# A hybrid decoder step on one core: 384 of 1056 tokens take their expert rows by indirect DMA, 672 stay dense, and the gates are stored by expert tile, key and token

## The chip, the cores and the metric

The kernel runs on one core of a Trainium2 chip. The metric is the device time of one execution in microseconds (us). Tensors are float32. Where this text says TensorE, VectorE, ScalarE, GpSimd and SyncE, the profile says PE, DVE, ACT, POOL and SP; PEld is TensorE's weight load.

## What is computed

One inference step of a decoder layer, for 1024 prompt tokens and 8 x 4 sample tokens (N = 1056), D = 1024. Three branches (a short convolution, a gated delta rule, a memory attention) are merged; then a product-key expert layer follows. The change is in that last layer alone:

```python
q = (xb @ w_q).reshape(blk, PEER_HEADS, 2, PEER_D_HALF)          # 8 heads
s = jnp.einsum('nhpd,phkd->nhpk', q, sub_keys)                   # 2 x 128 key scores
sv, si = lax.top_k(s, PEER_TOPK)                                 # 16 of each
...
eidx = jnp.take_along_axis(cidx, ti, axis=-1)                    # 16 of 16384 experts per head
gates = jax.nn.softmax(tv, axis=-1)
u = jnp.take(u_tab, eidx, axis=0)
act = jax.nn.gelu(jnp.einsum('nd,nhkd->nhk', xb, u), approximate=False)
coef = gates * act
y = jnp.einsum('nhk,nhkd->nd', coef, jnp.take(v_tab, eidx, axis=0))
```

So each token uses 8 x 16 = 128 rows of `u_tab` and 128 rows of `v_tab` (16384 x 1024 each), and the output is the residual plus y, normalised.

## The kernel before

Everything up to the expert layer (start-up, projections, attention, delta rule, merge) runs first and is not touched. The expert layer is dense: for all 128 tiles of 128 experts the kernel multiplies the tile's u rows with all 1056 tokens, applies Gelu, multiplies by a gate that is zero where the expert was not chosen, and multiplies with the tile's v rows. Every product is split into a rounded high part and a low part and takes three passes (high x high, high x low, low x high). The tokens go in three chunks of 352 columns (`NCH`, `CH`), so a tile costs 8 (`KT`) x 3 chunks x 3 passes = 72 matmuls of 128x352 on either side, 144 in all.

The layer has three stages.

- **Routing** (`top_experts`): for each of the 8 heads PE forms two query products (72 matmuls each, `product`, L2745), the scores (L2756), and, in between, the u product of two expert tiles (`act_tile`, `act_chunk`, L2572) whose Gelu values go to DRAM (`tmp_acts`). DVE finds the top 16 with max, find-index and match-replace instructions (L2872 to L2963), and POOL turns ranks into keys (L2689 to L2705). Twenty tiles are done here (`ROUTE_TILES`).
- **Spreading the gates** (`spread_gates`): for every token DVE writes two one-hot matrices, by second key (L3062) and by first key times gate (L3063), 128x128 each; PE multiplies them (`unit`, L3083, four tokens at a time), ACT copies the result out (L3104), and after every 48 tokens SP stores the block `tmp_gates[block, key, key, token]` (L3132), in which a partition's 128 x 48 values lie together. A round is two blocks, 24 units; 11 rounds do 1056 tokens and four u tiles each (`SPREAD_TILES` = 44).
- **Experts** (`experts`): 64 tiles have their Gelu values in DRAM (STASH), 64 are computed here (LIVE). A `turn` does two live u products and four v tiles in two `values` calls of two tiles (L3265). SP loads a tile's gates in 48-token pieces (L3200), the stashed values (L3206) and v rows (L3212); ACT rounds (L3320, L3325) and applies Gelu (L3333); DVE multiplies by the gate (L3389), forms the low parts (L3394, L3398) and adds the finished banks to `yT` (`sum_up`, L3405). At the end PE transposes the sums, ACT and DVE normalise, SP stores.

The u rows come in as rows of the table and must be transposed: `load_u` fetches 32x32 blocks with four DMAs per tile (L2546, runs of 128 B), `turn_u` transposes on DVE into PSUM (L2561), `raise_u` rounds (L2585) and `cut_u` subtracts (L2605).

Everything is ordered by hand: each engine runs its own program in order, and semaphores tie them. `next_u` on SP asks for a u tile as soon as its slot is free, and in the spreading stage stands on the same queue as the gate stores.

## Time and profile before

| | |
|---|---|
| time, median of 3 runs | 5763.18 us (5760.07 to 5764.72) |
| span of the profiled execution | 5757.6 us |
| PE busy | 5567.8 us (97%) |
| DVE busy | 3314.0 us (58%) |
| ACT busy | 1316.0 us (23%) |
| POOL busy | 854.3 us (15%) |
| moved by DMA | 584.45 MB, 102 GB/s over the span |

The profiled execution's own time is its span, 5757.6 us, from the first to the last instruction; the runs are about 5.6 us above it. Busy times are unions over an engine's instructions. Matmuls overlap in the records (each lasts about twice its distance to the next), so the cost of one is the distance between starts or a group's length divided by its count.

### The profile page before, as it was taken

Reading aid. Unit: us, or ns where it says so; the run is one execution under the profiler, and the core shown is the slowest. Engines: PE = TensorE matmul, PEld = TensorE weight load, DVE = VectorE, ACT = ScalarE, POOL = GpSimd, SP = SyncE. Lnnn points to the kernel's source line nnn. Section 1 sums busy time; section 2 is a strip of 40 time slices with the busy share of each in tenths; the row PEclk is TensorE's granted clock in tenths of the full one; section 3 lists DMA queues with packets and bytes.
Section 4 is the critical chain, followed back from the end, with each engine's and each line's share of the span. In section 5 each row is a group of like instructions: output and inputs, shape, how many; then the busy total and the mean of one; then the engine's idle time right before and its main releaser. Section 6 shows DMA issues by size and latency. Waiting matters only on the chain. (4 is left out here: it accounts for less than half of the span.)

```text
span 5757.6 us, 95894 instructions
## 1 busy us (share of the span) xinstructions
PE 5567.8 (97%) x35846; PEld 5444.1 (95%) x35846; DVE 3314.0 (58%) x7740; ACT 1316.0 (23%) x2393; POOL 854.3 (15%) x550
## 2 busy tenths in 40 slices
PE   8999999998998998999999998999999999999999
PEld 6999998986888997999999998999999999999998
DVE  3236402123766354799778885666666666666665
ACT  3013211122333013222333332112111112111122
POOL 0332323321221333355000000000000000000000
PEclk9999999999998998999999999999999999999999
DMA  4222224343111444222455666333443334443332
GB/s 159 63 63 92 97 88 112 110 154 111 49 45 60 140 123 125 63 63 53 126 154 147 167 158 172 89 89 91 96 101 89 89 89 93 102 94 89 89 89 83
DMA packets 1220496, 584.45 MB, mean 102 GB/s; under 512 B 915240, under 2 KB 1158952, under 8 KB 1217381
## 3 DMA queue, kind: packets, MB, share of 16 engines
q1 hardware_dynamic: 928800, 453.31, 30.1%
q10 hardware_dynamic: 290400, 124.94, 8.1%
q0 software_dynamic: 1152, 4.19, 0.3%
q8 instruction: 101, 1.65, 0.1%
q14 instruction: 43, 0.35, 0.0%
HBM read 410.77 MB, written 171.59 MB: 101 GB/s over the span
## 5 line engine op out<-in xcount | busy, mean ns | idle before, releaser
L3405 DVE TENSOR_TENSOR yT<-yT,ex_y 128x352 f32<-128x352 f32 x1512 | 787.9, 521 | 779.1 <-PE ex_y L3265 779.1
L2572 PE MATMUL ea_banks<-h_high,ea_uT_high 128*128 128x352 f32 x3072 | 1006.9, 328 | 22.6 <-PEq L3026 10.2
L2572 PE MATMUL ea_banks<-h_high,ea_uT_low 128*128 128x352 f32 x3072 | 990.5, 322 | 0.0
L2572 PE MATMUL ea_banks<-h_low,ea_uT_high 128*128 128x352 f32 x3072 | 989.2, 322 | 0.0
L3265 PE MATMUL ex_y<-ex_c_high,w_mb_high 128*128 128x352 f32 x3024 | 976.0, 323 | 4.9 <-DVE yT L3405 4.9
L3265 PE MATMUL ex_y<-ex_c_low,w_mb_high 128*128 128x352 f32 x3024 | 973.1, 322 | 0.0
L3265 PE MATMUL ex_y<-ex_c_high,w_mb_low 128*128 128x352 f32 x3024 | 971.8, 321 | 0.0
L2572 PEld LDWEIGHTS ea_banks<-h_high,ea_uT_high 128*128 128x128 f32 x3072 | 580.0, 189 | 23.7 <-issue 15.4
L2572 PEld LDWEIGHTS ea_banks<-h_low,ea_uT_high 128*128 128x128 f32 x3072 | 581.3, 189 | 0.0
L2572 PEld LDWEIGHTS ea_banks<-h_high,ea_uT_low 128*128 128x128 f32 x3072 | 579.5, 189 | 0.0
L3265 PEld LDWEIGHTS ex_y<-ex_c_high,w_mb_high 128*128 128x128 f32 x3024 | 568.4, 188 | 5.2 <-DVE yT L3405 5.2
L3265 PEld LDWEIGHTS ex_y<-ex_c_low,w_mb_high 128*128 128x128 f32 x3024 | 568.6, 188 | 0.0
L3265 PEld LDWEIGHTS ex_y<-ex_c_high,w_mb_low 128*128 128x128 f32 x3024 | 568.4, 188 | 0.0
L120 PE MATMUL p_in<-h_high,w_in_high 128*128 128x352 f32 x1536 | 495.5, 323 | 0.0
L120 PE MATMUL p_in<-h_low,w_in_high 128*128 128x352 f32 x1536 | 492.3, 320 | 0.0
L120 PE MATMUL p_in<-h_high,w_in_low 128*128 128x352 f32 x1536 | 491.8, 320 | 0.0
L3320 ACT CAST w_mb_high<-w_mb_raw 128x1024 fp32r<-128x1024 f32 x126 | 126.3, 1050 | 1398.5 <-PE ex_y L3265 1394.9
L120 PEld LDWEIGHTS p_in<-h_low,w_in_high 128*128 128x128 f32 x1536 | 288.6, 188 | 0.0
L120 PEld LDWEIGHTS p_in<-h_high,w_in_high 128*128 128x128 f32 x1536 | 288.1, 188 | 0.0
L120 PEld LDWEIGHTS p_in<-h_high,w_in_low 128*128 128x128 f32 x1536 | 287.8, 187 | 0.0
L3062 DVE TENSOR_SCALAR w_mb_raw<-iota,yT 128x128 f32<-128x128 f32 x704 | 197.4, 280 | 136.8 <-PE sg_ps L3083 135.5
L3063 DVE TENSOR_SCALAR w_mb_raw<-iota,yT 128x128 f32<-128x128 f32 x704 | 241.4, 343 | 0.0
(497 smaller groups left out, 9461.7 us busy)
## 6 DMA issues: line engine op xcount, KB each, us to landing
ex_gate<-tmp_gates SPq DMA_DIRECT2D x128, 528.0 KB, 6.2
w_mb_raw<-in_peer_v SPq DMA_DIRECT2D x128, 512.0 KB, 5.6
w_in_raw<-in_w_in SPq DMA_DIRECT2D x88, 512.0 KB, 3.8
ea_u_raw<-in_peer_u SPq DMA_DIRECT2D x268, 128.0 KB, 4.2
tmp_acts<-ea_coef ACTq DMA_DIRECT2D x64, 528.0 KB, 2.7
tmp_gates<-yT SPq DMA_DIRECT2D x11, 3072.0 KB, 9.4
tmp_gates<-sg_out SPq DMA_DIRECT2D x11, 3072.0 KB, 9.5
ex_kept<-tmp_acts SPq DMA_DIRECT2D x64, 528.0 KB, 7.0
```

Of the source, the lines that this page charges most:

```text
L120: last = pe.matmul(banks[0:rows, n, 0:CH], a[:, kk, 0:rows], b[:, kk, chunk(n)], start=(kk == 0 and a is wt.high[s] and b is high), stop=( ...
L2572: last = pe.matmul(acts.banks[:, n, 0:CH], a[:, c, :], b[:, c, chunk(n)], start=(c == 0 and a is acts.uT_high[s] and b is high), stop=(c = ...
L3062: dve.tensor_scalar(second_key[s][:, u, :], k["iota"][:, :], now[:, 1, at:at + 1], None, ALU.is_equal)
L3063: last = dve.tensor_scalar(first_key[s][:, u, :], k["iota"][:, :], now[:, 0, at:at + 1], now[:, 2, at:at + 1], ALU.is_equal, ALU.mult)
L3265: last = pe.matmul(ps_y[:, n, 0:CH], x[:, c, :], y[:, chunk(n)], start=(s == 0 and x is wt.high[0] and y is c_high[kind][0]), stop=(s == 1 ...
L3320: act.copy(v_high[s][:, :, :], v_raw[:, s, :, :]).then_inc(v_high_made, 1)
L3405: dve.tensor_tensor(at, at, ps_y[:, n, 0:CH], ALU.add).then_inc(summed, 1)
```

## The change

It splits the tokens. The first `GT` = 384 (three tiles of 128, one token per partition) leave the dense layer; the other `ND` = 672 stay in it in two chunks of 336 (`DC`, `CD`). For the 384 tokens the 128 expert numbers of each are kept as an index, and for slot j of a token tile one indirect DMA on POOL's queue fetches 128 rows of 4 KB, one per partition. DVE takes a dot product with the token's own row for u, and adds gate x Gelu x row for v. That is 3 x 128 u gathers and 3 x 128 v gathers; the 128 u gathers of the third token tile run in the spreading stage, the other 640 in the expert stage (20 in each of 32 turns, five row buffers).

Besides: u comes from a table that the host lays out transposed (`peer_uT`), so DVE's transposes and the four-part loads go; four instead of two u tiles are done per head (`HEAD_TILES`), 36 tiles in the routing stage and 28 in seven spreading rounds; a spreading unit's two one-hots of four tokens are one DVE instruction of 1024 elements, and POOL multiplies the first keys by the gates; `tmp_gates` is now `[expert tile, key, token]`; and the expert loop is 32 turns, in which the v products of the two stashed tiles and of the two live tiles of the turn before are summed in one bank before `sum_up` adds 672 columns.

The core of the diff (`SUMMED` is the token tile whose dots are made while spreading):

```diff
+G = 3
+GT = G * P
+ND = N - GT
+DC = 2
+CD = ND // DC
-ROUTE_TILES = 2 * H + 4
-SPREAD_TILES = 44
+HEAD_TILES = 4
+ROUTE_TILES = HEAD_TILES * H + 4
+SPREAD_TILES = 28
...
+def gather(pool, table, index, t, slot, row, landed):
+    pool.indirect_dma_start(row, None, table, bass.IndirectOffsetOnAxis(ap=index[:, t, slot:slot + 1], axis=0)).then_inc(landed, 16)
...
-    for j in range(SUB):
-        eng.dma_start(acts.u_raw[j * BLOCK:(j + 1) * BLOCK, s, :].rearrange("r (b c) -> r b c", c=BLOCK), rows[j]).then_inc(acts.u_in[s], 16)
+    eng.dma_start(acts.u_raw[:, s, :], io["peer_uT"][ds(e, 1), :, :].rearrange("o p c -> p (o c)")).then_inc(acts.u_in[s], 16)
...
@@ spread_gates, DVE
-                    for u in range(UN):
-                        at = r * UN + u
-                        dve.tensor_scalar(second_key[s][:, u, :], k["iota"][:, :], now[:, 1, at:at + 1], None, ALU.is_equal)
-                        last = dve.tensor_scalar(first_key[s][:, u, :], k["iota"][:, :], now[:, 0, at:at + 1], now[:, 2, at:at + 1],
-                                                 ALU.is_equal, ALU.mult)
+                    dve.tensor_tensor(keys[s], all_keys, own_keys, ALU.is_equal).then_inc(hot_made, 1)
+                    if r % (per_chunk * DC) == per_chunk:
+                        e, half, s = tile_of(i, r // (per_chunk * DC))
+                        cut_u(dve, acts, e + 1, 1 - s)
...
+                    for m in dots_after(r, first):
+                        dot(i, m, first)
@@ spread_gates, POOL (new)
+                for r in range(units):
...
+                    pool.wait_ge(hot_made, i * units + r + 1)
+                    pool.tensor_tensor(first_key, first_key, over_columns(chosen[:, 2, at:at + UN]), ALU.mult).then_inc(hot_weighed, 1)
+                    for m in dots_after(r, i == 0):
+                        if base + m + RING < P:
+                            pool.wait_ge(row_used, base + m + 1)
+                            gather_next(base + m + RING)
@@ spread_gates, ACT (every tile, at its first chunk)
-                            raise_u(act, acts, e + 1, 1 - s, 3 * e + 48)
+                            raise_u(act, acts, e + 1, half + s, 1 - s)
@@ spread_gates, SP
-                    sp.dma_start(tmp["gates"][ds(2 * i + bs, 1), :, :, :].rearrange("o j i n -> j (o i) n"), out[bs]).then_inc(stored[bs], 16)
+                    sp.dma_start(tmp["gates"][:, :, ds(2 * BT * i + bs * BT, BT)].rearrange("i j n -> j i n"), out[bs]).then_inc(stored[bs], 16)
@@ experts, SP
-                sp.dma_start(gate[:, slot, :].rearrange("p (b n) -> p b n", n=GATE_BLOCK),
-                             tmp["gates"][:, :, ds(tile_of(kind, g, s), 1), :].rearrange("b j o n -> j b (o n)")).then_inc(gate_in[slot], 16)
+                sp.dma_start(gate[:, s, :], tmp["gates"][ds(tile, 1), :, :].rearrange("o j n -> j (o n)")).then_inc(gate_in[s], 16)
@@ experts, POOL (new)
+                if nth >= RING:
+                    pool.wait_ge(row_used, nth - RING + 1)
...
+                gather(pool, table, gt.index, t, EACH * g + j, row[nth % RING], row_in[nth % RING])
@@ experts, DVE (new)
+                if m < U_ROWS:
+                    t, j = m // EACH, m % EACH
+                    dve.tensor_tensor_reduce(out=of, in0=of, in1=gt.h_row[t], scale=1.0, scalar=0.0, op0=ALU.mult, op1=ALU.add,
+                                             accum_out=dots[:, t, j:j + 1]).then_inc(row_used, 1)
+                else:
+                    t, j = (m - U_ROWS) % G, (m - U_ROWS) // G
...
+                    dve.scalar_tensor_tensor(out=gt.sum_row[t], in0=of, scalar=coefs[:, t, j:j + 1], in1=gt.sum_row[t],
+                                             op0=ALU.mult, op1=ALU.add).then_inc(row_used, 1)
@@ experts, ACT: the live coefficients of the turn before
+                act.wait_ge(l_weighed, 2 * g + s + 1)
+                if s == 0:
+                    act.wait_ge(multiplied, KT * (g + 1))
+                act.copy(l_high[s][:, :], acts.coef[:, s, :]).then_inc(l_high_made, 1)
```

Three places show what the program now issues. The first is SP's queue in a spreading round, around the store of the first block: before,

```order
L2546 DMA ea_u_raw<-in_peer_u 32x32x32
L3131 ISA
L3132 ISA
L3132 DMA tmp_gates<-yT 128x6144
L2546 ISA
L2546 DMA ea_u_raw<-in_peer_u 32x32x32
```

and with the change,

```order
L2584 DMA ea_u_raw<-in_peer_uT 128x1024
L3224 ISA
L3225 ISA
L3225 DMA tmp_gates<-yT 128x128x48
L2584 ISA
L2584 DMA ea_u_raw<-in_peer_uT 128x1024
```

The place is the same, but the store is 128x128 runs of 48 values, where it was one run of 6144 per partition, and the next u tile stands right behind it.

The second is POOL's queue at the start of the spreading stage, where it had nothing before (`picks` holds the gates and one of three row buffers, L3120 is the multiplication by the gates):

```order
L2576 DMA yT<-in_peer_u,gt_index 128x1024 x2
L2576 DMA picks<-in_peer_u,gt_index 128x1024
L3120 TENSOR_TENSOR w_mb_raw<-w_mb_raw,picks 128x512 x2
L2576 DMA yT<-in_peer_u,gt_index 128x1024
L3120 TENSOR_TENSOR sg_keys<-sg_keys,picks 128x512
L2576 DMA yT<-in_peer_u,gt_index 128x1024
```

Three gathers go ahead; after that gathers and multiplications alternate.

The third is DVE at the start of a turn of the expert loop (L3389 weighs by the gate, L3398, L3394 and L2605 are low parts): before,

```order
L3389 TENSOR_TENSOR ex_gate<-ex_gate,ea_coef 128x1056
L3397 ISA
L3398 TENSOR_TENSOR w_mb_low<-w_mb_raw,w_mb_high 128x1024
L3397 REGISTER_ALU
L3398 TENSOR_TENSOR w_mb_low<-w_mb_raw,w_mb_high 128x1024
L3382 ISA
L3389 TENSOR_TENSOR ex_gate<-ex_gate,ex_kept 128x1056
```

and with the change,

```order
L3569 TENSOR_TENSOR ex_l_low<-ea_coef,ex_l_high 128x672
L3593 ISA
L3597 ISA yT,ex_dots<-yT,h_high_plain 128x1024
L3597 ISA ex_dots 128x1
L3572 ISA
L3573 TENSOR_TENSOR w_mb_low<-w_mb_raw,w_mb_high 128x1024
L3572 REGISTER_ALU
L3573 TENSOR_TENSOR w_mb_low<-w_mb_raw,w_mb_high 128x1024
```

The turn begins with the live low parts of the turn before, and a dot product, which is two instructions (L3597, the second of one element), stands ahead of the v tiles' low parts.

## Rows read from the trace of the kernel before

**Rows 1.** Busy time of each engine by stretch: routing, spreading, start, loop and end of experts.
```profile
core 0: us, PE busy (x) PEld busy (x) DVE busy (x) ACT busy (x) POOL busy (x), PEclk, DMA share, GB/s
2261.00:2763.00 502.00, 466.39 (x2923) 458.53 (x2923) 417.66 (x1955) 118.52 (x231) 220.11 (x102) 0.96 0.29 63
2763.00:3506.00 743.00, 742.01 (x5278) 742.04 (x5279) 598.27 (x2255) 259.21 (x485) 0.00 (x0) 1.00 0.58 152
3506.00:3556.00 50.00, 31.28 (x169) 30.57 (x168) 16.11 (x17) 10.42 (x17) 0.00 (x0) 0.86 1.05 288
3556.00:5711.00 2155.00, 2155.00 (x13514) 2155.00 (x13513) 1370.68 (x2067) 394.63 (x559) 0.00 (x0) 1.00 0.39 92
5711.00:5757.00 46.00, 32.49 (x221) 30.93 (x219) 24.91 (x44) 13.29 (x28) 0.00 (x0) 0.93 0.26 95
```

**Rows 2.** The chain that ended last, two neighbouring pieces: start us, length us, what.
```profile
4024.75 11.47 PE ea_banks L2572 x72
4036.22 22.96 PE ex_y L3265 x144
```

**Rows 3.** Source L2954 (once per key and head): duration ns, first and last start.
```profile
L2954 DVE TENSOR_TENSOR picks<-iota,tk_rank x16: 2550/2556/2560, 2373.6 to 2741.9; 128x2304 f32<-128x2304 f32 x16
```

**Rows 4.** Groups by line in the routing stage: busy us, mean ns of one.
```profile
L2756 PE MATMUL tk_ps<-tk_keysT,tk_qT 128*128 (+1 forms) x288 | 34.7, 275 | 0.0
```

**Rows 5.** Timeline of DVE in the expert loop: start us, length us.
```profile
4025.23 1.25 DVE L3389 TENSOR_TENSOR ex_gate<-ex_gate,ex_kept 128x1056 f32<-128x1056 f32 x1
4026.40 2.35 DVE L3398 TENSOR_TENSOR w_mb_low<-w_mb_raw,w_mb_high 128x1024 fp32r<-128x1024 f32 x2
4028.67 1.25 DVE L3389 TENSOR_TENSOR ex_gate<-ex_gate,ea_coef 128x1056 f32<-128x1056 f32 x1
```

**Rows 6.** Timeline of DVE: an addition from PSUM, and a scalar-tensor-tensor.
```profile
5727.89 0.51 DVE L3463 TENSOR_TENSOR yT<-yT,ea_banks 128x352 f32<-128x352 f32 x1
5728.31 0.52 DVE L3463 TENSOR_TENSOR yT<-yT,ex_y 128x352 f32<-128x352 f32 x1
...
170.78 1.28 DVE L753 SCALAR_TENSOR_TENSOR conv_out<-conv_in,tap_now,conv_out 128x1024 f32<-128x1024 f32 x1
171.98 0.25 DVE L755 SCALAR_TENSOR_TENSOR conv_out<-conv_in_s,tap_now,conv_out 128x32 f32<-128x32 f32 x1
```

**Rows 7.** Source L3372: how long reading an accumulator out takes on ACT.
```profile
L3372 ACT ACTIVATION_READ_ACCUMULATOR ea_coef<-ea_t x3: 192/193/194, 5724.7 to 5748.0; 128x1 f32 x3
```

**Rows 8.** DMA by 2 us: v rows of 4 KB alone, then u and gate pieces; columns of Rows 1.
```profile
4036.00:4038.00 2.00, 2.00 (x15) 2.00 (x14) 0.52 (x1) 0.47 (x1) 0.00 (x0) 1.00 1.00 379
...
4030.00:4032.00 2.00, 2.00 (x15) 2.00 (x14) 2.00 (x3) 1.39 (x2) 0.00 (x0) 1.00 0.94 139
```

**Rows 9.** DMA queues: packets, MB, share of 16 engines; and the gates' store, KB, us to landing.
```profile
q1 hardware_dynamic: 928800, 453.31, 30.1%
q0 software_dynamic: 1152, 4.19, 0.3%
tmp_gates<-yT SPq DMA_DIRECT2D x11, 3072.0 KB, 9.4
```

**Rows 10.** POOL: a plain DMA of 128 rows of 4 KB, a multiplication, short copies.
```profile
L913 POOL DMA_DIRECT2D tmp_ym<-at_o x8: 844/844/992, 1239.0 to 1289.9; - x8
L1919 POOL TENSOR_TENSOR dp_qkv<-dp_qkv,dp_root_q x16: 1263/1272/1281, 1382.9 to 1776.0; 128x512 f32<-128x512 f32 x16
L908 POOL COPY at_qpad<-q_samples x32: 189/189/191, 1218.6 to 1222.5; 128x8 f32<-128x8 f32 x32
```

**Rows 11.** Timeline of DVE while routing: two casts of 144 elements.
```profile
2423.78 0.23 DVE L2936 CAST tk_rank_f<-tk_sums_at 128x144 f32<-128x144 uint32 x1
...
2444.33 2.63 DVE L2896 CAST tk_where<-tk_at 128x144 f32<-128x144 uint32 x1
```

**Rows 12.** Timeline of POOL at the second of these casts.
```profile
2441.72 5.14 POOL L2689 TENSOR_TENSOR picks<-picks,tk_where 128x2304 f32<-128x2304 f32 x1
```

More of the change, by code:

```diff
@@ L2621, in top_experts @@
+def top_experts(nc, k, io, tmp, high, low, room, picks, wt, acts, gt):
     HK = H * TOPK
@@ new lines, in dots_after, with _, gather_next @@
+        def dots_after(r, first):
+            total = FIRST if first else DOTS
+            return range(total * r // units, total * (r + 1) // units)
+        @block.gpsimd
+        def _(pool):
+            def gather_next(slot):
+                gather(pool, io["peer_u"], gt.index, SUMMED, slot, row[slot % RING], landed[slot % RING])
+            for slot in range(RING):
+                gather_next(slot)
+            for i in range(rounds):
+                base = FIRST + DOTS * (i - 1) if i else 0
+                for r in range(units):
+                    at = (i * units + r) * UN
+                    first_key = keys[r % SLOTS][:, 0, :, :]
+                    pool.wait_ge(hot_made, i * units + r + 1)
[4 more added lines that the diff above has]
+                            gather_next(base + m + RING)
@@ L3049, in _, with dot @@
         @block.vector
         def _(dve):
+            def dot(i, m, first):
+                base = 0 if first else FIRST + DOTS * (i - 1)
+                at = (0 if first else FIRST) + m
+                uses = at // RING if first else DOTS // RING * (i - 1) + at // RING
+                r = at % RING
+                dve.wait_ge(landed[r], 16 * uses + 16)
+                u_row = row[r].rearrange("p (c n) -> p c n", n=P)
+                dve.tensor_tensor_reduce(out=u_row, in0=u_row, in1=h_row[:, :].rearrange("p (c n) -> p c n", n=P), scale=1.0, scalar=0.0,
+                                         op0=ALU.mult, op1=ALU.add, accum_out=dots[:, m:m + 1]).then_inc(row_used, 1)
@@ L3235, in _ @@
+            for s in range(2):
+                load_gate(s, s)
+                if s == 0:
+                    load_kept(0, 0, None)
+                load_v(0, s, first=True)
+            sp.dma_start(gt.x2T, tmp["x2T"][:, :, 0:GT]).then_inc(x2_in, 16)
+            sp.dma_start(sumT, tmp["x2T"][:, :, GT:N]).then_inc(x2_in, 16)
+            load_kept(0, 1, 1)
+            turn(0)
+            with sp.Fori(1, turns - 1) as g:
                 turn(g)
-            load_gate(LIVE, pairs - 1, 1, 1)
@@ new lines, in _ @@
+            dve.wait_ge(acts.uT_high_made, FIRST_LIVE + 2)
+            dve.tensor_tensor(acts.uT_low[1][:, :, :], acts.u_raw[:, 1, :].rearrange("p (c n) -> p c n", n=P),
+                              acts.uT_high[1][:, :, :].bitcast(F32), ALU.subtract).then_inc(acts.uT_low_made, 1)
+            for s in range(2):
+                weigh_stash(0, s)
+            turn(0, first=True)
+            with dve.Fori(1, turns - 1) as g:
+                turn(g)
+            turn(LAST, last=True)
+            for s in range(2):
+                cut_live_v(LAST, s, acts.uT_high, acts.uT_low, acts.u_plain)
@@ L3467, in scale_out, with invert @@
+            for s in range(2):
+                cut_live(LAST, s)
+            def invert(size, t):
                 dve.wait_ge(out_rooted, t + 1)
```

859 lines of the change are left out of this document (492 added, 367 removed).

## The prediction

> **What bounds the kernel now.** All durations are from one profiled execution, whose own time is its span, 5757.6 us; the runs' median stands 5.6 us above it, and I add 5.6 at the end. A measurement of this kernel tells about 0.2% from no change, here 12 us.
>
> I read the stretches first [rows 1]. Spreading and the expert loop have PE busy for their whole length, with DVE at 81% and 64% and the DMA engines at 58% and 39%: PE sets 2898 us of the 3497 behind 2261. In routing PE has 466 of 502 us. The chain of waits says what PE does there: products of 72 or 144 matmuls end to end, 159.3 ns each [rows 2]. So fewer columns on PE shorten every stage until another engine is as full. The other views price the load that goes to DVE, POOL and the queues: sources and groups for routing [rows 3, 4], timelines for DVE [rows 5, 6], then DMA and POOL.
>
> **PE.** A column takes 1/2.4 ns at full clock, so 352 columns are 146.7 ns and 12.6 ns come on top of them. I keep those 12.6 for 336 columns: 152.6 ns (by plain proportion 152.1). One side of a tile goes from 72 matmuls, 11.47 us, to 48, 7.33 us. A turn has six sides (two u, four v), 288 matmuls, 43.9 us; 32 turns are 1406 us.
>
> **DVE in a turn.** 1024 elements from SBUF take 1.135 us (two instructions in 2.27 us, from the first's start to that of the next) and 1056 take about 1.17 [rows 5]; 352 from PSUM 0.42 by the distance of two starts; a scalar-tensor-tensor of 1024 1.20 [rows 6]. Between these, 672 elements are 0.76. The dot product with its sum is not in the trace. It is no shorter than a plain 1.135, and as two instructions perhaps the 1.20 and an accumulator read as on ACT, 0.19 [rows 7], 1.39. I take 1.35, since the order shows the second instruction. A turn: eight weighings and coefficient low parts 6.1, eight `sum_up` 6.1, six low parts of v and u 6.8, twelve v rows (12 x 1.20) 14.4, eight dots 10.8, small ones 0.2; 44.4 us in all (42.7 with the shortest dot). At a turn's end the last matmuls release both the last additions and ACT's rounding that DVE's next low part needs, so I add 1 us and more: about 46. DVE is as full as PE.
>
> **DMA in a turn.** With v rows alone in flight the engines are wholly busy at 379 GB/s [rows 8], 23.7 GB/s each, so a packet of 4 KB takes 173 ns. The turn moves 20 gathers, four v tiles and two u tiles, 26 transfers of 128 such rows, eight rows per engine: 36.0 us. Six gate and value tiles of 2688 B per partition, 117 ns in proportion, are 5.6. Together 41.6 us of 44: 90% or more of all engines, four times what the loop has now. The `ex` gates lose their short pieces, which helps; that is in the 5.6.
>
> POOL issues 20 gathers. Its one price is a plain DMA of 128 rows, 0.84 us [rows 10]: 17 us of a turn, hidden. ACT does what it did for fewer columns (395 us in the loop before) and is no limit.
>
> **The experts' stage.** PE 43.9, DVE 46 and DMA 41.6 in one loop of five row buffers, each waiting for the others at times: I take 48 us a turn, 1536, and 80 for the start, the last v products and the end (96 before): 1616 where 2251 stand.
>
> **Routing.** The period of a head is 52.2 us: the first of two L2954 of the first head starts at 2373.6 and the second of the last at 2741.9, 2.5 apart within a head and seven periods in all [rows 3]. PE's work in it was 22.9 (query products) + 22.9 (two u tiles) + 34.7/8 = 4.3 (scores [rows 4]), 50.1. With four tiles of 7.33 it is 56.5. DVE loses its transposes and gains two more low parts at 1.135, so it stays under 418/8 = 52 us a head [rows 1]. Period 57.5, so 7 x 5.3 = 37, less the shorter tiles beside the stage's ends: 538 us.
>
> **Spreading.** 743 us less 44 x 11.47 are 238 for 1056 tokens: 0.226 us a token on PE. A round of the seven is 96 tokens and four tiles: 21.7 + 29.3 = 51 us on PE. DVE has 24 one-hots of 1024 elements (1.18), 18.3 dots (128 over seven rounds, 24.7), four low parts 4.5 and little else: 58. POOL has 24 multiplications of 512 elements at 1.27 [rows 10] and 18.3 gathers, 46. It takes the first-key half of the hot work off DVE, and puts a step of 1.3 us between DVE and PE, covered by the double buffer while DVE runs ahead.
>
> The DMA part decides. The store was one run of 24 KB per partition and landed in 9.4 us; now its 3 MB are 16384 runs of 192 B, 1024 per engine. For their price: the hardware queues moved 928800 packets of 488 B on average in 30.1% of 16 x 5757.6 us [rows 9], 29.9 ns each; the line through this and the 4 KB packet gives 18.2 ns for 192 B. Pieces of 128 and 192 B read in the loop (139 GB/s at 0.94) bound it at 13.9 and 20.8 ns [rows 8]. One store: 18.6 us, two per round 37.3. With the gathers (18.3 x 1.385 = 25.3), u tiles 5.5 and values 3.8 the engines have 72 us of work in a round, already over PE and DVE.
>
> The order makes it worse. The u tile that stands behind a store on SP's queue is needed by ACT some six units (14.5 us) later, and ACT's program is in order, so a late tile holds the copies out of PSUM, then PE. Its packets stand behind the store's 18.6 us, shared with about seven gathers (9.7) and values (2): some 30 us from the store's issue. Then load 2.5, rounding 1, low part 1.1, three units of DVE 7, the last copy before the next store 1.5: half a round is about 43 us, a round 86, seven 602. The wait is what takes part of the gain back: 602 stands for 743 where DVE's 58 would give 406 plus ends.
>
> **Sum.** 2261 + 538 + 602 + 1616 = 5017 us of span, 5020 as a run, 12.9% less than now.
>
> **A rule of the Trainium skill against this change.** The last row of "Specifications" in "DMA: Bandwidth & Descriptors" asks at least 512 B of a transfer for full rate, and says that below it the engine reads, modifies and writes. No row here shows a short write. By the skill's rule the gate store is the one place that suffers; what it would do is the third rival.
>
> **Rivals.**
> *No stall in spreading.* The store's pieces interleave with the u tile, or the queue's 18 us are shorter (13.9 ns: 14 us), and the round is DVE's 58: 421 with its ends. If the turns too come at 46, 1552: 2261 + 538 + 421 + 1552 + 6 = 4778. For it: DVE and PE are within 15% and no store waits are seen now. Against: 72 us of DMA work is over 58.
>
> *The gathers are slow or disturb DVE.* The software queue took 0.3% for 1152 packets, 276 us, up to 0.24 us each (0.26 with the rounding) where 0.173 is the bare 4 KB [rows 9]. At 0.26 a turn's DMA is 56 us, and seven more rounds' worth of delay in spreading about 68: 5350. Or DVE stands still while POOL works: a cast of 144 elements took 0.23 us once and 2.63 at another time [rows 11], and the long one ended at 2446.96, just when POOL's 5.14 us multiplication ended, 2446.86 [rows 12]. If DVE's 26 operations with two SBUF inputs lose the 20 x 0.84 us that POOL issues, a turn is 62 us: 5470. Against the latter: in routing, where POOL is busy for 220 us, DVE fits its work in.
>
> "SBUF: two separate sides" in "SBUF — State Buffer" of the Trainium skill has the rule behind this: VectorE and GpSimd share a pair of ports as an exclusive lock for a whole instruction, for VectorE operations of two SBUF inputs only against a GpSimd one that reads SBUF. By that rule the cast's row fits as a case of the lock; whether the issue of a gather takes it, no row shows.
>
> *Short writes cost double.* 36.4 ns a piece, a store 37, half a round 61, a round 122, the stage 854: 5275.
>
> *Slower.* POOL's price for a gather decides. It works out 128 addresses from an index; a plain DMA's address steps need none of this. With g us for each of 768 gathers and POOL as the bound, a spreading round is 30.5 + 18.3 g and a turn 20 g; the total is 2261 + 538 + 7 x 30.5 + 80 + 768 g = 3093 + 768 g, and the change is slower from g = 3.47 us on. The nearest row for small work by POOL is 32 copies of 8 elements in 4 us [rows 10]; one such step per four addresses gives g = 4 and 6170 us. The low end is 0.84. I take the low end, the same kind of instruction and the same 128 rows.
>
> That the change doesn't do what it says is excluded by the order: three gathers ahead, alternating with POOL's multiplications, and two chunks for three.
>
> **Chances.** Forecast (a stall at the store, turns of about 48) 0.42; no stall 0.17; slow gathers or DVE disturbed 0.24; short writes at double price 0.08; slower 0.08; within 0.2% of now 0.01. The forecast's own range is 4880 to 5160. The 80% range reaches over the no-stall case and both forms of slow gathers: 4740 to 5480. PE's clock is a further risk: it was 0.86 where PE waited at the experts' start [rows 1], and stalls in spreading may lower it between 1.2 and 2.4 GHz; that is inside the range.
>
> **What the profile after would show.** Right: PE's tiles of 48 in 7.3 us; spreading near 600 us with PE busy for some 60%, the longest wait of PE or ACT traced to the u tile behind the store, which lands in about 30 us; turns of 48 us with PE, DVE and DMA all over 85%; routing periods of 57 us. Wrong: gathers over 0.85 us on POOL, dots far over 1.35 us on DVE, one-hots or low parts that stretch beside gathers, turns at one engine's pace with the others far below, a store under 15 us or over 35, or DMA at full share with under 300 GB/s in the turns.

## The result, and the profile after

| | before | after | forecast |
|---|---|---|---|
| median of 4 runs, us | 5762.14 (5760.07 to 5764.72) | 5028.80 (5021.81 to 5034.06) | 5020, 4740 to 5480 |
| ratio, 95% interval | | 0.8727 [0.8715, 0.8740] | 0.871 |
| span of the profiled execution | 5757.6 | 5022.3 | 5017 |
| routing | 502 | 605 | 538 |
| spreading | 743 | 550 | 602 |
| experts (start, loop, end) | 2251 | 1606 | 1616 |

The total is 9 us off, out of three stages of which two are off by 50 and more: routing takes 67 us more than forecast and spreading 52 less, and they cancel. The stretches of the changed kernel, with the columns of [rows 1]:

```profile
2261.00:2866.00 605.00, 524.36 (x3284) 515.95 (x3284) 428.23 (x1930) 139.93 (x236) 236.06 (x100) 0.93 0.20 67
2866.00:3416.00 550.00, 427.06 (x2695) 411.96 (x2694) 377.23 (x466) 147.77 (x256) 314.79 (x296) 0.85 0.96 241
3416.00:3466.00 50.00, 15.76 (x74) 15.52 (x75) 6.72 (x8) 7.33 (x11) 6.74 (x6) 0.57 0.99 259
3466.00:4974.00 1508.00, 1420.32 (x9027) 1402.53 (x9027) 1357.91 (x1613) 324.72 (x471) 936.76 (x633) 0.99 0.91 328
4974.00:5022.00 48.00, 30.43 (x191) 29.23 (x189) 31.74 (x46) 14.70 (x30) 2.32 (x2) 0.87 0.40 134
```

PE no longer fills spreading (78%) and is at 94% in the loop, where DVE has 90% and DMA 91%. PE's granted clock is 0.85 of 2.4 GHz in spreading, where it stands still in pieces, and 0.57 (between its two levels, 1.2 and 2.4 GHz) in the experts' start. Three lines of sources (duration of one in ns, first and last start), of which the first answers to [rows 3]:

```profile
L2994 DVE TENSOR_TENSOR picks<-iota,tk_rank x16: 2550/2554/2559, 2392.8 to 2844.3; 128x2304 f32<-128x2304 f32 x16
...
L3225 SPq DMA_DIRECT2D tmp_gates<-yT x7: 414/415/419, 2902.0 to 3375.5; - x7
...
L3573 DVE TENSOR_TENSOR w_mb_low<-w_mb_raw,w_mb_high x64: 1215/1221/1229, 3463.3 to 4944.5; 128x1024 fp32r<-128x1024 f32 x64
```

And the store by the page's list of DMA issues, 26.9 us to landing where [rows 9] has 9.4:

```profile
tmp_gates<-yT SPq DMA_DIRECT2D x7, 3072.0 KB, 26.9
```

From the sources' first and last starts come the three periods used below: a head (2844.3 - 2.5 - 2392.8)/7 = 64.1 us, a spreading round (3375.5 - 2902.0)/6 = 78.9 us, a turn (4944.5 - 3463.3 - 1.2)/31 = 47.7 us (the 1.2 is the distance of the two within a turn).

**Spreading, step by step.** SP's queue around two stores, by the timeline (start, length):

```profile
2943.18 0.41 SPq L3225 DMA_DIRECT2D tmp_gates<-sg_out  x1
2944.20 24.76 SPq L2584 DMA_DIRECT2D ea_u_raw<-in_peer_uT  x2
2983.10 0.41 SPq L3225 DMA_DIRECT2D tmp_gates<-yT  x1
2983.79 24.82 SPq L2584 DMA_DIRECT2D ea_u_raw<-in_peer_uT  x1
```

ACT in the same stretch; in brackets how long it stood idle before, and for what:

```profile
2956.15 0.59 ACT L3197 COPY yT<-sg_ps 128x512 f32<-128x512 f32 x1 [0.31 <-PE sg_ps L3177]
2972.37 1.04 ACT L2613 CAST ea_uT_high<-ea_u_raw 128x1024 fp32r<-128x1024 f32 x1 [15.64 <-DMA ea_u_raw<-in_peer_uT]
```

The store is issued at 2943.2; the two u loads behind it take 24.8 us to be issued, and the one behind the next store takes 24.8 alone (the median u load takes 0.33); ACT stands for 15.6 us and rounds the tile at 2972.4, 29.2 us after the store; the next store comes 10.7 us later. Forecast were 32.5 and 10.6.

### The profile page after: what moved, and what is told of

Its sections match the earlier page's. It is cut to its first block and busy times, and to the rows that moved or that the text cites. A ratio compares the mean times of both kernels' runs of the same rounds, so it can differ in the third digit from the quotient of the medians.

```text
span 5022.3 us, 76357 instructions
## 1 busy us (share of the span) xinstructions
PE 4559.0 (91%) x29021; PEld 4403.0 (88%) x29021; DVE 3088.2 (61%) x5466; ACT 1154.4 (23%) x2078; POOL 2131.5 (42%) x1486
## 3 DMA queue, kind: packets, MB, share of 16 engines
q0 software_dynamic: 111744, 406.90, 23.0%
## 5 line engine op out<-in xcount | busy, mean ns | idle before, releaser
L2601 PE MATMUL ea_banks<-h_high,ea_uT_high 128*128 128x336 f32 x2048 | 679.3, 332 | 116.7 <-DVE ea_uT_low L2631 49.5
L2601 PE MATMUL ea_banks<-h_high,ea_uT_low 128*128 128x336 f32 x2048 | 667.8, 326 | 0.0
L2601 PE MATMUL ea_banks<-h_low,ea_uT_high 128*128 128x336 f32 x2048 | 666.3, 325 | 0.0
L2576 POOL DMA_INDIRECT yT<-in_peer_u,gt_index x278 | 383.2, 1379 | 302.2 <-DVE h_low_plain L3603 117.7
L3416 PE MATMUL ex_y<-ex_l_high,ex_lv_high 128*128 128x336 f32 x992 | 319.0, 322 | 36.0 <-DVE ex_lv_low L3577 35.9
L3416 PE MATMUL ex_y<-ex_s_high,w_mb_high 128*128 128x336 f32 x1024 | 323.9, 316 | 5.2 <-DVE yT L3588 5.2
L3416 PE MATMUL ex_y<-ex_s_high,w_mb_low 128*128 128x336 f32 x1024 | 327.4, 320 | 0.0
L3416 PE MATMUL ex_y<-ex_s_low,w_mb_high 128*128 128x336 f32 x1024 | 324.5, 317 | 0.0
L3416 PE MATMUL ex_y<-ex_l_high,ex_lv_low 128*128 128x336 f32 x992 | 314.6, 317 | 0.0
L3416 PE MATMUL ex_y<-ex_l_low,ex_lv_high 128*128 128x336 f32 x992 | 314.2, 317 | 0.0
L3597 DVE CUSTOM_DVE_ANT_1 yT<-yT,h_high_plain 128x1024 f32<-128x1024 f32 x192 | 232.6, 1221 | 76.5 <-DMA yT<-in_peer_u,gt_index 76.2
## 6 DMA issues: line engine op xcount, KB each, us to landing
tmp_gates<-yT SPq DMA_DIRECT2D x7, 3072.0 KB, 26.9
```

The source lines that it names most:

```text
L2576: pool.indirect_dma_start(row, None, table, bass.IndirectOffsetOnAxis(ap=index[:, t, slot:slot + 1], axis=0)).then_inc(landed, 16)
L2601: last = pe.matmul(acts.banks[:, n, 0:CD], a[:, c, :], b[:, c, dense(n)], start=(c == 0 and a is acts.uT_high[s] and b is high), stop=(c = ...
L3416: last = pe.matmul(ps_y[:, bank, n, 0:CD], a[:, c, :], b[:, part_of(n)], start=(x == 0 and a is v_high and b is c_high), stop=(x == len(ti ...
L3597: dve.tensor_tensor_reduce(out=of, in0=of, in1=gt.h_row[t], scale=1.0, scalar=0.0, op0=ALU.mult, op1=ALU.add, accum_out=dots[:, t, j:j + 1 ...
```

## The experiments

Medians are of 4 runs each (e13: 10), ratios against the kernel before on the same chip (5759 to 5761 us).

**e1: the u tile ahead of the store.**

```diff
-    for j in range(TILES // 2 * bs, TILES // 2 * bs + TILES // 2):
-        next_u(sp, acts, io, ROUTE_TILES + 2 + TILES * i + j, j % 2)
+next_u(sp, acts, io, ROUTE_TILES + 2, 0)
...
+    half_round(i, 0, (1, 2))
+    half_round(i, 1, (3, 4))
```

> In the spreading stage SP asks for each u tile one place earlier, ahead of the gate store behind which it stood; nothing else is changed. Changed kernel: 5028.8 us, stores 78.9 us apart per round. My theory (the u tile behind the 3 MB store holds ScalarE, then TensorE): the stall goes and the round is set by what is next, the 72 us of DMA work or VectorE's 58 us: 58 to 74 us a round, so 5 to 21 us less in each of seven, 4880 to 4995 us. Rival (the DMA engines are simply full for the whole round, whatever the order): 79 us a round as before, within 10 us of 5029.

4925.5 us, ratio 0.8548 [0.8534, 0.8562]: 103 us less. The stores' first and last start, and the stretch between them in the columns of [rows 1]:

```profile
L3224 SPq DMA_DIRECT2D tmp_gates<-yT x7: 304/414/872, 2903.6 to 3285.9; - x7
```
```profile
2904.00:3286.00 382.00, 331.50 (x2303) 322.60 (x2302) 322.41 (x398) 124.54 (x216) 271.35 (x253) 0.96 1.19 299
```

A round is (3285.9 - 2903.6)/6 = 63.7 us, 15.2 less; seven make 106. PE's clock is back at 0.96. The order was the price, as forecast, and full DMA engines were not: their share is higher now (it can pass 1, as in [rows 1]), at 299 GB/s.

**e2: the store in one run per partition.** The gates stand in DRAM in another order than they are read, so the dense part's result is another.

```diff
-tmp["gates"][:, :, ds(2 * BT * i + bs * BT, BT)].rearrange("i j n -> j i n")
+tmp["gates"].rearrange("i j n -> (i j n)").rearrange("(b j x) -> b j x", j=P, x=P * BT)[ds(2 * i + bs, 1), :, :]
```

> The gate store keeps its size and place but is written as one run of 24 KB per partition, as the kernel before wrote it (so the gates in DRAM stand in the wrong order and the output is not the reference's). Theory (the store's 16384 short pieces cost 18 us and more of all engines, and with the u tile behind it the stall): the store lands in under 14 us, a round falls from 79 to VectorE's 58 to 62 us, 4890 to 4925 us. Rival (a round is bound by VectorE and GpSimd taking turns, not by the store): a round of 75 us or more, 5000 to 5029 us.

4923.3 us, 0.8543 [0.8529, 0.8557]; the store lands in 11.7 us where the changed kernel's takes 26.9, a round is 65.1 us (stores at 2904.0 and 3294.4, six rounds apart). The layout costs as much as the order did, 14 us a round, and my 58 to 62 was too low by 3.

```profile
tmp_gates<-yT SPq DMA_DIRECT2D x7, 3072.0 KB, 11.7
```

**e3: no gathers and no dots in spreading** (the u products of the third token tile are left out).

```diff
-                    for m in dots_after(r, first):
-                        dot(i, m, first)
...
-                            gather_next(base + m + RING)
```

> Leaves out the 128 gathers and the 128 dot products of the spreading stage (the third token tile's u products are then not computed); the store stays in short pieces. Theory (store and u tile behind it set half a round, gathers lengthen the store): the store lands in 19 to 21 us and half a round falls by 8 to 10 us to about 30, a round from 79 to 58 to 64, now near TensorE's 51: 4880 to 4925 us. Rival (the store alone, by the price of its pieces, holds the round, gathers are free beside it): 74 us or more, over 4990 us.

4898.1 us, 0.8500 [0.8486, 0.8514]. The store's landing and its starts:

```profile
tmp_gates<-yT SPq DMA_DIRECT2D x7, 3072.0 KB, 20.1
```
```profile
L3214 SPq DMA_DIRECT2D tmp_gates<-yT x7: 414/415/419, 2902.8 to 3264.4; - x7
```

The store alone lands in 20.1 us, 6.8 less than with gathers beside it; the forecast had 18.6 and 30. A round is 60.3 us. So both the short pieces and the gathers lengthen the store. The 60.3 us are not the gathers' alone, for the run leaves out DVE's dots too (DVE is busy for 199 of the 361 us from 2903 to 3264). Taking the short pieces away, or gathers and dots, or moving the load ahead, takes 14 to 19 us off a round.

**e4: the low part inside the selection.** In routing of the changed kernel DVE makes the fourth tile's low part ahead of the selection; here it stands in its middle.

```diff
-                odd_tile(h, 1)
                 if not first:
                     weigh(h - 1, own)
-                select(h, own, first=first)
+                select(h, own, between=lambda: odd_tile(h, 1), first=first)
```

The rows that led to it are waits of the changed kernel in one head, 2552 to 2616 (us in total, times, longest), and the windows in which PE stood:

```profile
DVE ea_uT_low L2631 <- ACT ea_uT_high L2613: 12.6, 1, 12.6
...
PE ea_banks L2601 <- DVE ea_uT_low L2631: 4.7, 1, 4.7
```
```profile
2600.00:2604.00 4.00, 0.90 (x9) 0.70 (x7) 4.00 (x26) 2.98 (x5) 3.82 (x2) 0.88 0.00 0
2604.00:2608.00 4.00, 2.40 (x9) 2.41 (x9) 4.00 (x4) 0.49 (x1) 3.64 (x3) 0.50 0.32 114
```

DVE stood still for 12.6 us, then was late with the first low part of the next head while PE waited, and PE's clock fell to 0.50 of 2.4 GHz, its lower level, for the first matmuls after that.

> In the routing stage the low part of the fourth u tile of a head is made on VectorE in the middle of the selection instead of ahead of it, where VectorE stood still for 12.6 us until ScalarE had rounded the tile. Changed kernel: 64.1 us a head where 57.5 were forecast. Theory (that idle time makes the next head's first low part late, and TensorE waits for it at the head's start): the wait shrinks by 8 us or more, a head falls to 57 to 60 us, 4990 to 5005 us. Rival (VectorE and GpSimd disturb each other, the order is innocent): 63 us or more a head, within 8 us of 5029.

4969.9 us, 0.8627 [0.8612, 0.8641]: 59 less. The source that marks the heads:

```profile
L2994 DVE TENSOR_TENSOR picks<-iota,tk_rank x16: 2549/2555/2559, 2389.7 to 2789.2; 128x2304 f32<-128x2304 f32 x16
```

A head is (2789.2 - 2.5 - 2389.7)/7 = 56.7 us, 7.4 less, and equal to PE's work of 56.5. That is slightly better than the 57 to 60 expected, and the time is 20 us under the band of 4990 to 5005. The order was the whole of what the period lost.

The rival, that VectorE and GpSimd disturb each other, is refuted as the cause of the long period, but the disturbance is there. The low parts in the routing stage (duration of one in ns: shortest, median, longest), in the kernel before and in the changed one, and POOL and DVE around the late low part:

```profile
L2605 DVE TENSOR_TENSOR ea_uT_low<-ea_t,ea_uT_high x38: 674/679/686, 2327.0 to 2745.0; 128x512 fp32r<-128x512 f32 x38
```
```profile
L2631 DVE TENSOR_TENSOR ea_uT_low<-ea_u_raw,ea_uT_high x35: 1217/1468/6078, 2299.7 to 2846.8; 128x1024 fp32r<-128x1024 f32 x35
```
```profile
2601.78 2.60 POOL L2717 TENSOR_TENSOR picks<-picks 128x1152 f32<-128x1152 f32 x1 [0.18 <-POOL picks L2713]
2604.56 2.17 POOL L2717 TENSOR_TENSOR picks<-picks 128x576 f32<-128x576 f32 x1 [0.18 <-POOL picks L2717]
```
```profile
2603.22 4.59 DVE L2631 TENSOR_TENSOR ea_uT_low<-ea_u_raw,ea_uT_high 128x1024 fp32r<-128x1024 f32 x2
```

Before, a low part had one input in PSUM (`ea_t`, where the transposes went) and did not stretch, even where POOL's same operation (then L2693) ran beside it. Since u comes in transposed, both inputs are in SBUF, and beside POOL's operations on SBUF the 35 of them take 62.8 us where 35 undisturbed ones of 1.22 would take 43. At 2603.22 two take 4.59 us (2.35 elsewhere): the first is done at 2605.6, when PE starts, 1.2 us after POOL's first operation ended at 2604.38. That is some 1.2 of the 4.7 us that PE waited. In e4 they stretch even more, 2.14 us in the mean, and the period is PE's all the same.

**e5: both moves.** The edits of e1 and e4 together.

> Both moves of order together: the u tile ahead of the gate store (alone 4925.5 us, 103 less than the changed kernel) and the low part inside the selection (alone 4969.9 us, 59 less). Theory (two waits in two stages that have nothing to do with each other): the gains add, 4860 to 4875 us. Rival (both take the same slack, for instance TensorE's clock or tiles that one stage hands the other late): 4890 us or more.

4861.1 us, 0.8444 [0.8429, 0.8458]. Alone they give 103 and 59, in sum 162, together 168: they add. The stretches of routing and spreading:

```profile
2261.00:2808.00 547.00, 510.11 (x3284) 503.92 (x3285) 424.96 (x1931) 138.40 (x233) 232.03 (x102) 0.96 0.22 75
2808.00:3255.00 447.00, 390.55 (x2679) 379.40 (x2678) 376.42 (x463) 148.10 (x255) 314.96 (x295) 0.94 1.15 293
```

**e6, e7, e8: what sets a turn.** Each takes work from one engine in the turns of the changed kernel: e6 the dots from DVE (the u products of two token tiles are left out), e7 half of every gather from DMA and POOL (half of each row tile is old), e8 one of three passes of the v products from PE (less exact).

```diff
-dve.tensor_tensor_reduce(out=of, in0=of, in1=gt.h_row[t], ...)
+dve.tensor_copy(dots[:, t, j:j + 1], row[r][:, 0:1]).then_inc(row_used, 1)
```
```diff
-gather(pool, table, gt.index, t, EACH * g + j, row[nth % RING], row_in[nth % RING])
+index = bass.IndirectOffsetOnAxis(ap=gt.index[0:P // 2, t, EACH * g + j:EACH * g + j + 1], axis=0)
+pool.indirect_dma_start(row[nth % RING][half, :], None, table, index).then_inc(row_in[nth % RING], 16)
```
```diff
-for a, b in ((v_high, c_high), (v_high, c_low), (v_low, c_high)):
+for a, b in ((v_high, c_high), (v_low, c_high)):
```

> In the expert turns each of the eight dot products (1.3 us) is replaced by a copy of one column (0.1 us or less), gathers and buffers unchanged; the u products of two token tiles are then not computed. VectorE's work in a turn falls from 44 to 35 us, TensorE's stays 43.9, the DMA engines' 41.6. Theory (VectorE, TensorE and DMA are nearly level, and the 4.4 us over TensorE's work are waits at the turn's edge in which VectorE's order has a part): a turn falls from 48.3 to 45.5 to 47 us, 4940 to 4990 us. Rival (VectorE is the bound): a turn of 44.5 us or less, under 4910 us. Rival (VectorE has no part in it): within 15 us of 5029.

> In the expert turns each gather fetches 64 rows instead of 128 (to the lower and the upper half of the partitions in turn; the other half of the products is then made of old rows). DMA work in a turn falls from 41.6 to about 28 us and POOL has half as many addresses; VectorE and TensorE do as much as before. Theory (at 91% the DMA engines are full but not what ends the turn): a turn of 46.5 to 48, 4970 to 5020 us. Rival (the DMA engines set the turn): 46 us or less, 4955 us or less.

> In the v products of the turns the pass of the rounded v rows with the low part of the coefficients is left out (the output is less exact): 64 of 288 matmuls, 9.8 us of TensorE's 43.9 us in a turn. Theory (VectorE's 44.4 us with its wait at the edge, and 41.6 us of DMA, stand right behind TensorE): a turn falls only to 45.5 to 47 us, 4940 to 4990 us. Rival (TensorE alone sets the turn): 38.5 to 42 us, 4720 to 4830 us. Rival (TensorE is not the bound at all): 5015 us or more.

| | time, us | ratio, interval | turn, us | busy time less than in the changed kernel, us a turn |
|---|---|---|---|---|
| changed | 5028.8 | 0.8727 [0.8715, 0.8740] | 47.7 | |
| e6 | 4962.0 | 0.8617 [0.8603, 0.8632] | 45.6 | 7.8 of DVE |
| e7 | 4970.1 | 0.8636 [0.8621, 0.8650] | 45.8 | 5 of DMA |
| e8 | 5002.1 | 0.8688 [0.8673, 0.8702] | 46.9 | 7.1 of PE |

All turns are read from the v low parts' first and last start, as above. The last column is the engine's share of the rows below times the turn, against the changed kernel's; expected were about 9, 13.6 and 9.8 us. Ten turns of each, in the order changed, e6, e7 and e8:

```profile
3900.00:4383.00 483.00, 455.82 (x2909) 450.41 (x2908) 433.00 (x516) 103.43 (x150) 300.26 (x203) 1.00 0.91 328
```
```profile
3900.00:4383.00 483.00, 474.37 (x3054) 471.32 (x3053) 371.00 (x460) 111.84 (x163) 287.88 (x214) 1.00 0.94 344
```
```profile
3900.00:4383.00 483.00, 472.34 (x3041) 469.11 (x3040) 454.33 (x536) 108.95 (x158) 284.12 (x211) 1.00 0.84 226
```
```profile
3900.00:4383.00 483.00, 390.90 (x2288) 372.14 (x2288) 440.69 (x522) 105.33 (x152) 302.65 (x204) 0.94 0.92 332
```

No engine alone sets the turn. With DVE or DMA relieved PE comes to 98% and stops the gain after 2 us; with 64 of PE's 288 matmuls gone only 0.8 are gained. PE's clock falls there to 0.94 of 2.4 GHz, from 1.00, and gives a part of its relief back (7.1 us less busy for 9.8 of work). So what stands on top is DVE with its waits, and PE is 2 us behind. e6 came as expected. e7's time of 4970 is at the edge of what I expected, but its turn of 45.8 is under my 46.5 and where the rival had it: the row transfers have a larger part than I had given them. The DMA share fell far less than the bytes (0.91 to 0.84, 328 to 226 GB/s). Whether bytes or latency made the gain it doesn't tell, since a half gather also comes sooner (5.7 us to landing in the median, 7.2 over all whole ones); e10 bears on it. e8 gained less than the least I expected (5002 against 4940 to 4990): PE was less of a bound than "43.9 us plus waits" says.

**e10: plain rows instead of gathered ones in the turns** (wrong rows, same bytes).

```diff
-gather(pool, table, gt.index, t, EACH * g + j, row[nth % RING], row_in[nth % RING])
+at = nth % (NE // P) * P
+pool.dma_start(row[nth % RING], table[at:at + P, :]).then_inc(row_in[nth % RING], 16)
```

> In the expert turns POOL issues a plain DMA of 128 neighbouring rows in place of each indirect one, same bytes, same buffers (the rows are then the wrong ones). Changed kernel: turns 47.7 us apart; the shortest gather on POOL 0.94 us, many 1.2 to 2.0. Theory (an index costs POOL 0.1 us over the plain 0.84, the rest of a long gather is a wait for VectorE's instruction, and scattered rows cost the DMA engines no more than neighbouring ones): POOL's shortest 0.84, long ones still 1.1 to 1.9, the turn within 0.5 us, 5010 to 5035 us. Rival (scattered rows or the index are dear): a turn of 46.5 us or less, under 4990 us.

4944.2 us, 0.8585 [0.8570, 0.8599]: 85 less, where I expected nothing. The turn is 44.9 us. The bytes are the same, and still the turn falls by 2.8 us, more than with half the rows: how soon the rows come has the larger part. Here they land in 6.5 us in the median and POOL issues one in 0.54. Three timelines: POOL in the changed kernel, DVE in the same moments, and POOL in e10:

```profile
4008.30 1.74 POOL L2576 DMA_INDIRECT ea_u_raw<-in_peer_v,gt_index  x1 [4.67 <-DVE h_low_plain L3603]
...
4012.59 1.74 POOL L2576 DMA_INDIRECT yT<-in_peer_v,gt_index  x1 [0.65 <-DVE h_low_plain L3603]
...
4016.60 0.94 POOL L2576 DMA_INDIRECT yT<-in_peer_v,gt_index  x1 [0.31 <-issue]
```
```profile
4006.75 2.48 DVE L3603 SCALAR_TENSOR_TENSOR h_low_plain<-ea_u_raw,ex_coefs,h_low_plain 128x1024 f32<-128x1024 f32 x2
...
4011.04 2.48 DVE L3603 SCALAR_TENSOR_TENSOR h_low_plain<-yT,ex_coefs,h_low_plain 128x1024 f32<-128x1024 f32 x2
...
4016.60 0.84 DVE L3588 TENSOR_TENSOR yT<-yT,ex_y 128x672 f32<-128x672 f32 x1
```
```profile
4012.86 0.54 POOL L3380 DMA_DIRECT2D ea_u_raw<-in_peer_v  x1 [0.61 <-DVE ex_dots L3598]
4016.27 0.54 POOL L3380 DMA_DIRECT2D ea_u_raw<-in_peer_v  x1 [2.88 <-DVE ex_dots L3598]
```

An indirect DMA that starts while DVE is in a scalar-tensor-tensor of two SBUF inputs ends 0.8 us after that instruction (4010.04 after 4009.23, 4014.33 after 4013.52), and so do those that start in a low part or a dot of the turns (once a turn one sits through the two instructions that follow as well and takes 3.1 us); one that starts with an addition from PSUM takes 0.94. The plain DMA takes 0.54, at most 0.61, whatever DVE does. The Trainium skill has it so in "SBUF: two separate sides" of "SBUF — State Buffer": VectorE with two SBUF inputs and a GpSimd instruction that reads SBUF exclude each other for a whole instruction. This trace agrees for the indirect form in one direction, a gather waits for VectorE's instruction to end; that VectorE waits for a whole gather it does not show, for the two instructions at 4011.04 start inside the gather from 4010.35 to 4011.94 and keep their 2.48 us. Beside gathers the one that pays is POOL; beside POOL's own operations on SBUF it is DVE too (the low parts under e4).

The spreading stage shows the other side: there DVE's one-hots and dots have an input in PSUM (`sg_now`, `sg_h`), and the gathers beside them take 0.98 us. The long one, 1.79 us, starts in a low part, whose inputs are both in SBUF:

```profile
L2576 POOL DMA_INDIRECT yT<-in_peer_u,gt_index x82: 982/982/1787, 2884.0 to 3392.8; - x82
L2576 POOL DMA_INDIRECT picks<-in_peer_u,gt_index x41: 982/982/984, 2881.8 to 3386.4; - x41
```

**e14: the indirect form, but neighbouring rows.** The index is overwritten at the end of routing.

```diff
+for t in range(G):
+    last = dve.tensor_scalar(rows[:, t, 0, :], k["iota"][:, :], float(P), rows[:, 1, 1, 0:1], ALU.mult, ALU.add)
...
 dve.tensor_copy(gt.index[:, :, :], rows[:, 0:G, 0, :])
```

> The run with plain rows on POOL had turns of 44.9 us where the changed kernel has 47.7, and my forecast for it fell. It differed in two things: the form of the instruction (POOL 0.54 us each, never longer, against 0.94 to 3.1) and where the rows lie. Here the indirect instruction stays and only the index is set (four small instructions at the end of routing) so that each gather fetches 128 neighbouring rows (the wrong ones), as the plain DMA did. Theory (POOL's indirect instruction, which waits for VectorE's and makes rows late, is the whole difference): turns of 47.2 to 47.8 us, 5005 to 5035 us. Rival (rows scattered over the table are the price): turns of 45.5 us or less, under 4965 us. In between: each has a share.

5009.7 us, 0.8688 [0.8672, 0.8703]; turns (4937.6 - 3477.7 - 1.2)/31 = 47.1 us (routing ends 14.8 us later in its profile than in the changed kernel's, but 14.6 of them stand before the expert layer, which the edit doesn't touch, so turns are what is compared). The time is in my band, the turn just under it. Its rows, with the changed kernel's ahead, for one kind of gather:

```profile
L2576 POOL DMA_INDIRECT ea_u_raw<-in_peer_v,gt_index x192: 935/1599/1986, 3471.7 to 4974.6; - x192
```
```profile
L2576 POOL DMA_INDIRECT ea_u_raw<-in_peer_v,gt_index x192: 934/1605/1988, 3486.2 to 4968.1; - x192
```

POOL is the same. So of the 2.8 us between the changed kernel and e10, scattering makes 0.7 and the form of the instruction 2.1, each from one profile. How the later gathers become a longer turn was read, not tried: from 3900 to 4383 DVE waits 2.5 us a turn for a row of u and 1.7 for stashed values in the changed kernel, 1.6 and 0.04 in e10. Why the stashed values come sooner there stays open.

**e12: one more move, in the turns.** On top of e5.

```diff
                     for s in range(2):
                         cut_live(g - 1, s)
+                    take_rows(g - 1, ROWS - 1, ROWS)
...
                 sum_up(g, 6)
+                take_rows(g, v + 9, ROWS - 1)
                 if not last:
                     weigh_stash(g + 1, 1)
-                take_rows(g, v + 9, ROWS)
                 sum_up(g, 7)
```

> Both moves of order of the run before (4861.1 us) and one more in the turns: VectorE takes two v rows ahead of the weighing that waited 1.7 us for its values, and the last v row of a turn only after the next turn's coefficient low parts, for which ScalarE's Gelu and then TensorE wait (2.8 us a turn in TensorE's and its weight load's rows, 1.5 to 1.7 of it this). Theory (at the turn's edge VectorE is late by its own order): the turn falls from 47.5 by 1 to 2 us, 4800 to 4832 us. Rival (the DMA engines at 91% decide when rows and tiles are there, VectorE waits for them elsewhere): within 15 us of 4861.

4835.5 us (4829.1 to 4839.1), 0.8397 [0.8383, 0.8411]: 26 less than e5, and 193 less than the changed kernel. The turn falls by 1.0 us from e5's 47.4 to (4749.9 - 3308.6 - 1.2)/31 = 46.5. Three waits over ten turns of e12. In e5 the wait of ACT's Gelu for the low part was 25.8, PE's wait for that Gelu 9.6 and DVE's for the values 15.0 (in the changed kernel 33.6, 14.7 and 17.3); here the last two are gone, and the wait for v rows in the second line is new:

```profile
DVE yT L3602 <- DMA yT<-in_peer_u,gt_index: 22.4, 10, 2.7
...
DVE h_low_plain L3608 <- DMA ea_u_raw<-in_peer_v,gt_index: 7.9, 11, 1.2
...
ACT ea_coef L3496 <- DVE ex_l_low L3574: 6.0, 8, 0.8
```

The edge is cured; a part of the gain comes back as waits for gathered v rows. The total is 4 us beyond the band I gave.

**e13: the gate layout alone, in the kernel before.**

```diff
-tmp["gates"][ds(2 * i + bs, 1), :, :, :].rearrange("o j i n -> j (o i) n")
+tmp["gates"][:, :, ds(2 * BT * i + bs * BT, BT)].rearrange("i j n -> j i n")
```

> The kernel before with one part of the change alone: its gates stored by expert tile, key and token (16384 runs of 192 B per store) and loaded as one run per partition. A round there is 67.5 us, all TensorE. Theory (a store then lands in about 19 to 24 us, under half a round of 33.8, with no gathers beside it; the u tile behind it comes late only by a few us, and the expert loop is bound by TensorE): 0 to 10 us a round lost, 5750 to 5830 us. Rival (the stall at the store is the layout's alone): 15 us a round or more, over 5860 us. Rival (the contiguous loads give something back in the loop): under 5745 us.

5765.9 us, ratio 1.0010 [1.0000, 1.0019]: 6 us more, near what the measurement tells. The spreading stage, and the store:

```profile
2763.00:3506.00 743.00, 742.03 (x5278) 741.82 (x5278) 597.77 (x2255) 259.47 (x484) 0.00 (x0) 1.00 0.97 152
```
```profile
tmp_gates<-yT SPq DMA_DIRECT2D x11, 3072.0 KB, 19.3
```

The DMA share goes from 0.58 [rows 1] to 0.97 for the same bytes, the store from 9.4 to 19.3 us, and the stage does not lengthen: PE covers it. The 6 us can be read behind it: between the stages, where the last store has to land, PE stands for 19.8 us instead of 10.2. The contiguous loads give nothing back, since there too PE is the bound. So the layout cost 6 us at most until the change took PE's cover away.

## Why the prediction was right, and where it was not

- **PE per matmul** (152.6 ns, 7.33 us a tile side): right. With the waits cured, a head is 56.7 us for 56.5 of work.
- **Routing, 538: wrong, 605.** The failed step is "PE's work in it ... With four tiles of 7.33 it is 56.5 ... Period 57.5". The sum of PE's work was right, and DVE's nearly (428 us of the stage, where I had said under 418); what it left out is the order: twice as many low parts stand in DVE's program, one at a place where ACT is 12.6 us behind. Wait and clock made 7.4 us a head (e4). The low parts' 1.135 was short too: with both inputs in SBUF they take 1.8 us in the mean beside POOL. I had argued that DVE fits its work in beside POOL in routing; the low parts of the kernel before could, since they read PSUM. Some 20 us more fell before the first head's ranks, which I had not grown at all: L2994 starts at 2392.8 instead of 2373.6 [rows 3].
- **Spreading, 602: mechanism right, size 52 too high.** From store to u tile was 29.2 us where I had 30 + 2.5, the rest of the half 10.7 for 10.6; a half is 39.5 us, not 43. The 3.3 us, 14 times, are 46 of the 52. The piece of 192 B was sized well: 18.6 forecast, 20.1 us measured without gathers. What I called packets standing behind packets shows in the trace at the issue: SP needs 24.8 us to issue the load. PE is busy for 78% of the stage, not for some 60%: its work was right, but at 0.85 of 2.4 GHz it takes longer.
- **Turns, 48: right at 47.7**, with parts that were off. The dot takes 1.15 us from start to start, not 1.35 (below, its two instructions in DVE's timeline), so DVE has 433/483 x 47.7 = 42.8 us of a turn, not 44.4. In place of that stand waits that I had not named, 4.7 us a turn from 3900 to 4383: 2.5 for u rows, 1.7 for stashed values and 0.5 for ACT. The 48 was also partly luck, since the dot was sized too long and these waits too short. I had said "90% or more" of the DMA engines (0.91), and e7 shows their part.

```profile
4043.53 1.22 DVE L3597 CUSTOM_DVE_ANT_1 yT<-yT,h_high_plain 128x1024 f32<-128x1024 f32 x1
4044.68 0.08 DVE L3597 DVE_READ_ACCUMULATOR2_ANT ex_dots<- 128x1 f32 x1
4044.68 1.22 DVE L3597 CUSTOM_DVE_ANT_1 yT<-yT,h_high_plain 128x1024 f32<-128x1024 f32 x1
```

- **POOL's gather: under-sized.** "I take the low end", 0.84; it is 0.94 alone and 1.4 on average. Gathers over 0.85 us stood among my signs of being wrong, and they came. That stayed hidden on POOL (62% busy), but not in the turn: the form of the instruction is 2.1 us of it by e10 and e14, 67 us in 32 turns. That it acts through rows that come late to the ring of five fits the waits and was not tried. The rival with a disturbed DVE had the right pair of engines and, in the turns, the wrong loser: DVE's instructions keep their length, POOL waits. Where it looked, in routing, DVE does lose.
- **The other rivals.** Packets of 0.26 us on the software queue: refuted; 23.0% of 16 x 5022.3 us over 111744 packets are 165 ns each. Short writes at double price (37 us a store, the mechanism to which the Trainium skill's row in "Specifications" of "DMA: Bandwidth & Descriptors" pointed): refuted, 18.3 us at the least and 20.1 without gathers. The row's other half, that short pieces miss the full rate, this case has: 3072 KB in 20.1 us are 157 GB/s. No stall: its 58 us a round was not reached even in e3 (60.3) or e1 (63.7). What sets those 63.7 us is open: PE is at 87%, DVE at 84%, POOL at 71%. Slower: g would have had to be 3.47 us.
- **Two slips in the working, which leave the forecast's sum as it is:** 117 ns for a packet of 2688 B is the line through two prices, and in plain proportion it is 113; and 0.3% rounded up to 0.35% gives 0.28 us a packet on the software queue, not 0.26 (measured 0.165).

So the total was right by luck: routing's 67 us too many met 52 and 10 too few. The mechanisms of two stages were right; that of the third, an order in which DVE stands still and PE with it, was missing.

## What to carry to other kernels

A work item that an in-order engine or queue gets more of must be looked at for its place, not only its sum: two moves of a few lines gave 168 us here, which no sum of work shows. What stands behind a store of many short runs on one queue waits for its issue, so prefetches go ahead of it; and such a layout looks free as long as another engine covers it (e13). Where GpSimd issues indirect DMAs beside VectorE instructions with two SBUF inputs, count the longer issue in the latency of the buffers, even if GpSimd is far from full. And where a change moves an input of VectorE from PSUM to SBUF, look at what GpSimd does beside it: a low part of 1.22 us became 1.8 in the mean of the routing stage.

## What the runs showed of the hardware that was not expected

- A load behind the store of 16384 runs took 24.8 us to issue on SP, where the median u load took 0.33; with that store in the kernel before, up to 16.7 us for the u loads behind it (4.9 with the old layout).
- VectorE's subtraction of 1024 elements with both inputs in SBUF: 1.22 us, up to 6.1 beside GpSimd's operations in routing; with one input in PSUM, 512 elements: 0.67 to 0.69, beside the same operations.
- An indirect DMA of 128 rows: 0.94 us, up to 3.1 beside VectorE with two SBUF inputs, 0.98 beside VectorE with one in PSUM; a plain one of the same size in the same place: 0.54, at most 0.61.
- Rows scattered over the table cost 0.7 us in a turn of 20 gathers, against neighbouring ones (47.7 and 47.1, one profile each).
- Gathers of 64 rows relieve the DMA engines by less than their bytes: the mean packet of the software queue takes 18.3% x 16 x 4967.1 / 70784 = 205 ns there, 165 with 128 rows, and the share falls from 0.91 to 0.84 while the rate falls from 328 to 226 GB/s.
